# The dense feed-forward of layer 0 as Strassen's seven half-size products, with the weight sums made on VectorE

## The reference, cut to what matters

```python
D_MODEL = 1024
D_FF = 2816

def swiglu(h, wg, wu, wd):
    return (jax.nn.silu(h @ wg) * (h @ wu)) @ wd

    # layer_forward, layer 0: x = x + gt2 * swiglu(h2, w_ff_gate, w_ff_up, w_ff_down)
```

## Time and profile before

| | |
|---|---|
| time, median of 3 runs | 1638.91 us (1638.71 to 1642.12) |
| span of the profiled execution | 1643.6 us |
| TensorE busy in it | 1601.4 us (97%) |
| VectorE, ScalarE, GpSimd busy | 414.5, 150.2, 69.6 us |
| memory traffic | 535 MB, mean 326 GB/s |

### The profile page before, as it was taken

One profiled execution on the slowest core, in us unless ns is written; L12 is line 12 of the kernel. 1 busy time (PEld: TensorE's weight loads), 2 busy tenths in 40 slices (PEclk: granted clock), 3 DMA queues, 4 the chain that ended last, 5 costly groups with the idle time before them and its releaser, 6 DMA issues.

```text
span 1643.6 us, 34513 instructions
## 1 busy us (share of the span) xinstructions
PE 1601.4 (97%) x15756; PEld 1002.9 (61%) x15756; DVE 414.5 (25%) x877; ACT 150.2 (9%) x364; POOL 69.6 (4%) x118
## 2 busy tenths in 40 slices
PE   7999999999999999999999999999999999999997
PEld 3778887888886888863444444444554555555544
DVE  4468353101103794441111001100110011011132
ACT  2102301000002112130000000000000000000000
POOL 1111500000000010001000000000000000000010
PEclk8999999999999999999999999999999999999999
DMA  9998878564348877348999999999999999999995
GB/s 364 365 374 303 284 255 258 163 201 145 123 159 285 272 256 230 128 134 343 404 418 418 404 417 404 418 418 404 418 416 404 412 393 418 418 399 418 411 386 186
DMA packets 188920, 535.14 MB, mean 326 GB/s; under 512 B 13047, under 2 KB 113189, under 8 KB 175970
## 3 DMA queue, kind: packets, MB, share of 16 engines
q1 hardware_dynamic: 173298, 497.20, 79.9%
q0 software_dynamic: 8768, 28.96, 5.0%
q10 hardware_dynamic: 6704, 6.72, 1.3%
HBM read 517.47 MB, written 15.82 MB: 324 GB/s over the span
## 4 chain that ended last, share of the span: by engine, by line
PE 81%; DMA 12%; DVE 4%; SPq 1%; issue 1%; ACT 0%; POOL 0%; DVEq 0%
PE bank L1465 30%; PE bank L1486 14%; PE bank L1109 11%; PE bank L1022 10%; DMA ring<-in_w_exp_up 9%; PE bank L1322 5%; PE bank L1298 3%; PE bank L1286 2%; PE bank L1030 1%; DMA ring<-in_w_ada 1%; DVE inv L1922 1%; DMA w_route<-in_w_router 1%; PE bank L1273 1%; SPq L591 1%; PE bank L1124 1%
## 5 line engine op out<-in xcount | busy, mean ns | idle before, releaser
L1465 PE MATMUL bank<-ring,area 128*32 128x448 f32 x3072 | 302.9, 539 | 3.5 <-DMA ring<-in_w_exp_up 3.2
L1465 PE MATMUL bank<-ring,xT 128*32 128x448 f32 x3072 | 301.7, 539 | 3.6 <-DMA ring<-in_w_exp_up 3.4
L1109 PE MATMUL bank<-hT,ring 128*128 128x264 f32 x1024 | 239.3, 389 | 0.8 <-ACT hT L814 0.8
L1486 PE MATMUL bank<-area 128*32 128x256 f32 x3840 | 227.8, 379 | 1.2 <-issue 1.0
L1109 PEld LDWEIGHTS bank<-hT,ring 128*128 128x128 f32 x1024 | 193.4, 191 | 36.4 <-issue 4.5
L1465 PEld LDWEIGHTS bank<-ring,area 128*32 128x32 f32 x3072 | 109.8, 110 | 165.0 <-issue 157.8
L1465 PEld LDWEIGHTS bank<-ring,xT 128*32 128x32 f32 x3072 | 111.0, 110 | 162.6 <-issue 154.7
L1486 PEld LDWEIGHTS bank<-area 128*32 128x32 f32 x3840 | 139.2, 110 | 100.0 <-issue 44.3
L496 DVE TENSOR_TENSOR area<-bank,area 128x448 f32<-128x448 f32 x48 | 45.9, 956 | 577.5 <-ACT area L981 577.5
L1022 PE MATMUL bank<-hT,ring 128*128 128x264 f32 x704 | 157.4, 386 | 0.0
L1022 PEld LDWEIGHTS bank<-hT,ring 128*128 128x128 f32 x704 | 133.7, 190 | 23.2 <-issue 0.4
(11 more groups left out here) (314 smaller groups left out, 882.1 us busy)
## 6 DMA issues: line engine op xcount, KB each, us to landing
ring<-in_w_exp_gate SPq DMA_DIRECT2D x128, 896.0 KB, 18.2
ring<-in_w_exp_up SPq DMA_DIRECT2D x128, 896.0 KB, 20.0
area<-in_w_exp_down SPq DMA_DIRECT2D x64, 1024.0 KB, 18.3
ring<-in_w_ada SPq DMA_DIRECT2D x96, 512.0 KB, 10.4
ring<-in_w_in SPq DMA_DIRECT2D x32, 1024.0 KB, 12.5
ring<-in_w_exp_down SPq DMA_DIRECT2D x32, 1024.0 KB
area<-in_w_exp_down SPq DMA_DIRECT2D x32, 512.0 KB
ring<-in_w_ff_gate SPq DMA_DIRECT2D x22, 512.0 KB, 7.3
```

The costliest lines, as they stand in the source:

```text
L1109: mm = pe.matmul(bank[b][:, 0:T], w[:, c, :], hT[:, c, :], start=(c == 0), stop=(c == DC - 1))
L1465: mm = pe.matmul(bank[t + 3 * half][32 * g:32 * g + 32, 0:SLICE], tokens[:, t, 32 * r:32 * r + 32], w[half][:, SLICE * g:SLICE * (g + 1)], ...
L1486: mm = pe.matmul(bank[6 + t // 2][32 * q:32 * q + 32, (t % 2) * S:(t % 2 + 1) * S], FFN["actT"][:, m % 2, t, 32 * i:32 * i + 32], wide(at) ...
```

## The change: what it does

The two matrices of each product are cut in halves both ways: 256 hidden channels (two chunks) by 1024 input channels, and the tokens into 2 x 132. Four quarter products of each quarter of the result need 8 half-size products; the seven of Strassen's scheme (in Winograd's form) do with sums of quarters as operands. A half-size product has 128 x 128 weights over 132 tokens. Output columns come in `units` of two chunks: unit 2i is gate chunks 2i and 2i+1, unit 2i+1 the same of up (22 units of 7 products of 4 matmuls), and 4 units of the down product (7 products of 11 matmuls), which contracts all 22 hidden chunks at once, so that the groups and `fT` are gone. Before it was 16 matmuls over 264 tokens for each gate or up unit and 44 for each down unit.

Products of a unit are numbered 1, 2, 5, 6, 3, 7 and the fourth; `left(u)` and `right(u)` are the two banks of unit u, 132 columns each, one of three pairs. 1, 6, 7 and the fourth accumulate in `left`, 2 alone and then 5 and 3 in `right`; VectorE and ScalarE take partial sums out in between. VectorE makes three sums of weight quarters into `w_sum` and a fourth over its place in the page (`sum_pair` for a pair of units, `sum_down` for a down unit), one pair ahead, and once the four sums of `hT` quarters (`h_sum`, in `sq`) and three or four of the activations (`act_sum`). Gate, up and down pages come two at a time. The read of `mod` for layer 1 moves a little. Layer 1's first modulation waits for 14 of the 16 `x_new`, its sums of squares use bank 2 instead of 1, and ScalarE no longer waits for all of `x_new` before it starts the norm of layer 1. Some semaphores are shared now; one of these adds a wait: VectorE's bias rows at the start also wait for the constants' transfer.

```diff
-FF_GROUPS = (6, 6, 5, 5)
+HALF = T // 2
+DOWN_UNITS = 4
...
+                for j in range(0, FF_CHUNKS, 2):
+                    for kind, w in (("gate", A["w_ff_gate"][0]), ("up", A["w_ff_up"][0])):
+                        yield (kind, l, j), cols(w, j, 2)
+                        yield (kind, l, j + 1), None
+                for j in range(DOWN_UNITS):
+                    for q in range(3):
+                        rows = slice(q * DC * P, min((q + 1) * DC, FF_CHUNKS) * P)
+                        yield ("down", l, 6 * j + 2 * q), cols(A["w_ff_down"][0][rows, :], 2 * j, 2)
+                        yield ("down", l, 6 * j + 2 * q + 1), None
...
# TensorE
+            def product(out, w, x, first, last=True):
+                n = len(w)
+                for c in range(n):
+                    mm = pe.matmul(out, w[c], x[c], start=(first and c == 0), stop=(last and c == n - 1), skip_group_check=True)
+                return mm
...
+                def five_six(u):
+                    w5, w6 = summed(u // 2, 0), summed(u // 2, 1)
+                    pe.wait_ge(s.w_summed, 4 * (u // 2) + 1)
+                    pe.wait_ge(s.c11_read, u + 1)
+                    if u == 0:
+                        pe.wait_ge(s.h_summed, 1)
+                    product(right(u), [w5[:, u % 2, c, :] for c in range(4)], with_sums(0), True).then_inc(s.product_mm, 1)
...
+                    pe.wait_ge(s.w_summed, 4 * (u // 2) + 2)
+                    pe.wait_ge(s.one_kept, u + 1)
...
+                def fourth(u):
+                    pe.wait_ge(s.c22_read, u + 1)
...
+                first_two(0)
+                first_two(1)
+                five_six(0)
+                three_seven(0)
+                five_six(1)
+                fourth(0)
+                for u in range(1, FF_UNITS - 1):
+                    first_two(u + 1)
+                    three_seven(u)
+                    five_six(u + 1)
+                    fourth(u)
...
+                for u in range(a, a + DOWN_UNITS):
+                    down_middle(u)
+                    if u + 2 < a + DOWN_UNITS:
+                        down_pages(u + 2)
+                        down_one(u + 2, every)
+                    down_fourth(u)
+                    if u + 2 < a + DOWN_UNITS:
+                        down_two(u + 2, every)
...
# VectorE
+                        a11, a12, a21, a22 = v[:, 0:4, 0:P], v[:, 4:8, 0:P], v[:, 0:4, P:2 * P], v[:, 4:8, P:2 * P]
+                        if k == 0:
+                            r = dve.tensor_tensor(out, a21, a22, ALU.add)
+                        elif k == 1:
+                            r = dve.tensor_tensor(out, s1, a11, ALU.subtract)
+                        elif k == 2:
+                            r = dve.tensor_tensor(out, a12, s2, ALU.subtract)
+                        else:
+                            r = dve.tensor_tensor(a21, a11, a21, ALU.subtract)
...
+                for k in range(4):
+                    sum_pair(0, k)
+                b11, b12, b21, b22 = hs[:, 0:4, 0:HALF], hs[:, 0:4, HALF:T], hs[:, 4:8, 0:HALF], hs[:, 4:8, HALF:T]
+                dve.wait_ge(s.h_ready, 2 * DC)
+                for k, x, y in ((0, b12, b11), (1, b22, h_sum[:, 0, :, :]), (2, b22, b12), (3, b21, h_sum[:, 1, :, :])):
+                    if k in (1, 3):
+                        dve.wait_ge(s.h_summed, 1 + k // 2)
+                    dve.tensor_tensor(h_sum[:, k, :, :], x, y, ALU.subtract).then_inc(s.h_summed, 1)
+                read11(0, FF0["got_c"][:, 0, 0, 0:HALF])
+                for i in range(FF_PAIRS):
+                    u, g = 2 * i, FF0["got_c"][:, i % 2, :, :]
...
+                    read11(u + 1, even[:, 0:HALF])
+                    if i:
+                        more(0)
+                    read12(u, g[:, 0, HALF:T])
+                    read22(u, g[:, 1, HALF:T])
+                    if i == 0:
+                        more(0)
+                    more(1)
+                    if i < FF_PAIRS - 1:
+                        read11(u + 2, FF0["got_c"][:, (i + 1) % 2, 0, 0:HALF])
+                    more(2)
+                    read12(u + 1, even[:, HALF:T])
+                    read22(u + 1, odd[:, HALF:T])
...
+                    step(dve.tensor_tensor(even, even, g[:, 0, :], ALU.mult))
...
+                    step(dve.tensor_tensor(odd[:, HALF:T], odd[:, HALF:T], g[:, 1, HALF:T], ALU.mult))
+                    step(dve.tensor_tensor(act_sum[:, i, 0, :], even[:, HALF:T], even[:, 0:HALF], ALU.subtract))
+                    step(dve.tensor_tensor(act_sum[:, i, 2, :], odd[:, HALF:T], even[:, HALF:T], ALU.subtract))
+                    step(dve.tensor_tensor(act_sum[:, i, 1, :], odd[:, HALF:T], act_sum[:, i, 0, :], ALU.subtract))
+                    more(3)
+                    last_quarter(i)
...
# layer 1
                 if l:
+                    pe.wait_ge(s.x_new, DC + DC - 2)
                     for n in range(16, 24):
                         modulation(1, n, 0)
```

More of the change, by code:

```diff
@@ L302, in build @@
         DOWN_ROWS = ((0, 1), (2, 3), (4, 5), (6,), (7, 8), (9, 10), (11,), (12, 13))
-        PAIRED = ("z", "branch", "out")
-        SUM_BANK = (1, 3, 1, 7)
+        PAIRED = ("z", "branch", "out", "gate", "up", "down")
+        SUM_BANK = (1, 3, 2, 7)
         BIAS_BANK = (6, 7, 1, 5)
@@ L379, in used_up, with pages_at, summed, down_summed @@
             return number[(kind, l, i)] + 1
+        def pages_at(kind, i):
+            at, count = arrives[number[(kind, 0, i)]]
+            return pair_cols(at), page_in[at], count
+        def summed(i, k):
+            at = 4224 * (i % 2) + 1024 * k
+            return w_sum[:, at:at + 1024].rearrange("p (u c n) -> p u c n", u=2, c=4)
+        def down_summed(j, k):
+            at = 4224 * (1 - j % 2) + FF_PAIRS * P * k
+            return w_sum[:, at:at + FF_PAIRS * P].rearrange("p (c n) -> p c n", c=FF_PAIRS)
+        def product_order():
+            yield from ((1, 0), (2, 0), (1, 1), (2, 1), (5, 0), (6, 0), (3, 0), (7, 0), (5, 1), (6, 1))
+            for u in range(1, FF_UNITS - 1):
+                yield from ((1, u + 1), (2, u + 1), (3, u), (7, u), (5, u + 1), (6, u + 1))
+            first = FF_UNITS
+            yield from ((3, first - 1), (7, first - 1), (1, first), (2, first), (1, first + 1), (2, first + 1))
+            for u in range(first, first + DOWN_UNITS):
+                yield from ((5, u), (6, u), (3, u), (7, u))
+                if u + 2 < first + DOWN_UNITS:
+                    yield from ((1, u + 2), (2, u + 2))
+        finished = {product: n + 1 for n, product in enumerate(product_order())}
+        def left(u):
+            return bank[u % 3][:, 0:HALF]
+        def right(u):
+            return bank[3 + u % 3][:, 0:HALF]
         def experts(dve, step, f, act_t, silu, add_f, read_mod):
@@ L916, in _, with keep_five @@
                     touch(ACT.Silu)
[L917 to L924 removed]
+                    def keep_five(u):
+                        act.wait_ge(s.product_mm, finished[5, u])
+                        if u >= 2:
+                            act.wait_ge(s.c22_read, u - 1)
+                        act.copy(kept5[u % 2], right(u)).then_inc(s.five_kept, 1)
@@ new lines, in keep_two, with keep_one, silu_last @@
+                    def keep_two(u):
+                        act.wait_ge(s.product_mm, finished[6, u])
+                        if u >= 2:
+                            act.wait_ge(s.c12_read, u - 1)
+                        act.copy(kept2[u % 2], left(u)).then_inc(s.two_kept, 1)
+                    def keep_one(u, out):
+                        act.wait_ge(s.product_mm, finished[1, u])
+                        act.copy(out, left(u)).then_inc(s.one_kept, 1)
+                    def silu_last(i):
+                        act.wait_ge(s.pages_used, used_up("gate", 0, 2 * i + 1))
+                        act.activation(FF0["got_c"][:, i % 2, 1, 0:HALF], left(2 * i), ACT.Silu).then_inc(s.silu_out, 1)
@@ L1015, in page, with page_pair @@
                 return slot(n % RING)
[L1017 to L1021, removed]
-                    mm = pe.matmul(out, w[:, c, :], x[:, c, :], start=(c == 0), stop=(c == DC - 1))
-                mm.then_inc(s.pages_used, 1)
+            def page_pair(kind, i):
+                n = used[0]
+                assert stream[n][0] == (kind, 0, i)
+                at, count = arrives[n]
+                pe.wait_ge(page_in[at], count)
+                used[0] += 2
+                return pair_cols(at)
@@ L1962, in _ @@
                 if l == 0:
[L1963 to L1983 removed]
+                    feed_forward()
                 else:
```

439 lines of the change are left out of this document (323 added, 116 removed).

## The result

The changed kernel takes 1621.3 us (median of 4 runs, 1619.38 to 1627.39) against 1638.81 us: a ratio of 0.9897, 95% interval 0.9872 to 0.9922. Forecast were 1617.1, range 1612 to 1627. In a second measurement of both it is 0.9896 (0.9879 to 0.9914). The profiled execution has a span of 1625.7 us, 17.9 less than before's.

What follows compares the result with a forecast made beforehand. TensorE's stream of matmul records bounds the feed-forward: 209.4 + 4.5 + 0.5 + 0.2 = 214.6 against 235.15 us, -20.5, with -1.3 at the end -21.8, so 1638.9 becomes 1617.1 us; range 1612 to 1627.

Steps and rivals of the forecast that it cites:

- The pace: Feed-forward matmuls on TensorE: 1848 records of 132 columns at 0.1133 us each, 209.4 us, read from four records.
- The rival of the load as the pace: Feed-forward: weight loads set the record spacing; slower above 0.125 us each, 1759 us at 0.190; chance 0.11.
- The rule of the Trainium skill: Feed-forward matmuls: load and matmul together set the spacing, giving 0.164 us a record and a stage of 303 us.
- VectorE: Gate and up pairs: 10.4 us of VectorE work hides under TensorE's 12.7; as bound, with late pages, chance 0.09.
- The start: Feed-forward start: TensorE waits 4.5 us before product 5 of unit 0 for VectorE's sums and `read11`.
- The clock: After the feed-forward's starting stall: ten microseconds at half clock lose 5.1 us, time 1622.2; chance 0.30.
- the case without: The forecast itself, no clock fall after the feed-forward's starting stall: 1617.1 us; chance 0.46.
- the wait of 2.2 us at 58 us: Near the kernel's start: a single TensorE wait of 2.2 us that did not take the clock to half.
- Small stalls: Feed-forward: 0.5 us for some 180 hand-overs between TensorE and VectorE, from nothing to above 3 us.
- The end: Feed-forward's end to `z`: -1.3 us from the squares' wait; nothing counted for `z` pages, late by up to 1 us otherwise.
- The squares' wait: Layer 1's modulation: TensorE's 1.29 us wait for ScalarE's squares goes, -1.3 us.
- Given back later: Expert stage: its transfers, at 0.99, set the end and the gain is lost, 1637 to 1639 us; chance 0.04.

Runs made afterwards that it cites:

- The doubled sums: Changed kernel with VectorE making one, or two, weight sums twice per pair of units after the first; 1626.03 and 1636.06 us, one run each.
- the stream of 96 columns: Changed kernel with gate and up products streaming 96 of their 132 columns, part of the result not computed; 1630.5 us in one run.

## Why the prediction was right

**The pace.** Right, and to the point on which all hung: 0.1125 measured against 0.1133, 1848 x 0.1125 = 207.9 against 209.4 us. Four records were, here, enough to read it from. The rival of the load as the pace falls, with a margin that I did not see: at 0.1117 the load is the next bound. The rule of the Trainium skill ("TensorE: Matmul & The Clock Gate", "Back-to-back issue gap"), from which 0.164 came as an estimate, does not hold for these 32-bit passes: the trace has 0.1125.

**VectorE.** Right: no wait in the pairs. Its work is smaller than I said, 134 us in the stretch and not 150. The doubled sums show some 1.8 us in hand in a pair where my sum had 2.3 (12.7 less 10.4): with less work than I said VectorE is nearer to being the bound, so waiting in its order counts too, not its work alone.

**The start.** The wait was 3.8 instead of 4.5 us, and its cause as told.

**The clock.** This is the rival that came true, in smaller size: after the wait the clock fell, but for 3.4 us and not for 10, which costs 1.7 and not 5.1. With the same wait it fell in six of seven profiled executions (for 3.4 or 6.8 us), and in one it did not; I gave 0.30 beside 0.46 for the case without. One argument of mine was chance: that the wait of 2.2 us at 58 us "did not do it". Near there seven of the twelve profiled executions wait for 1.7 to 2.2 us, and in two of them, after waits of 1.82 and 1.94 us, the clock falls. After the change:

```profile
57.90 0.63 PE L1464 MATMUL bank<-cst,area 120*128 120x120 f32 x4 [1.82 <-DMA w_route<-in_w_router]
```
```profile
59.00:62.30 3.30, 3.30 (x30) 1.53 (x23) 0.52 (x3) 0.00 (x0) 0.00 (x0) 0.50 1.07 384
```

**Small stalls.** 0.5 us was said; the last two down units each wait 0.55 us (0.39 of it idle) for `read22`, since no product stands between their seventh and fourth. In the walk through VectorE's order I had looked at pairs and at the length of a down unit, not at this hand-over.

**The end.** Here a step failed, as I put it: "3 MB in the 12 us before `z` starts ... I count nothing; late by up to 1 us otherwise." The squares' wait went as predicted (-1.3), and with GpSimd's loads away the way is 11.8 us. But I did not count GpSimd's loads (1.3 MB), whose release, the last `x_new`, now comes right after the last record instead of after `add_f`. The pages ahead of `z` I counted rightly for the kernel after, four, but misread for the one before: its three were issued before the last record. That alone did not matter: with GpSimd's loads away the four are still issued after the end and `z` waits for `hT` again, and with the slots given back earlier, but the loads where they were, the wait stays. The wait is 4.5 us, and the clock falls after it once more, 1.7 us. In the prediction's own terms the end is +2.4 + 1.7 instead of -1.3, 5.4 us off. The other terms together are 0.5 us off (215.1 against 214.6 for the stretch), and that is luck in part: the shorter pace (1.5) and wait (0.7) stand against the clock (1.7) and the two hand-overs (1.1 where I had 0.5).

So the stages that the change touches give -16.0 us in the profile and not -21.8. The medians differ by 17.5, the spans by 17.9, since the first and the last row of the table add -1.9, which I had no term for and which no run puts down to the change. That the forecast is only 4.2 us off and not nearly 6 is luck as well.

**Given back later.** No: from the fourth `z` column to the experts' part it takes the same to 0.1 us, and the experts' part is not longer.

Open: why the clock stays in one execution out of seven after an equal wait and falls in two of seven after a shorter one; and how much of 3.1 us in the experts' part is more than chance.

## What to carry to other kernels

Halving the columns of a matmul pays only while its stream is longer than the load of its weights: here 132 columns are about the last that do, so seven products of half size win. The same scheme once more inside would not, by an estimate: it needs 1848 x 7/4 = 3234 records of 66 columns, and at 0.1117 us each, the pace of the loads, these take 361 us. When a stage ends earlier for one engine, list every queue that its last semaphore releases, GpSimd's too, and ask what they send at the moment the next stage's pages are due. Where an engine must prepare operands before a stage, let it make them in the order in which they are used.

## What the runs showed of the hardware

A load of 128 x 128 32-bit weights, shown with 190 ns, repeats every 0.1117 us in the stream of 96 columns, under matmuls on the same rows. After waits of 3.8 us with full work on both sides TensorE's granted clock went to its lower level, 1.2 GHz, for 3.4 or 6.8 us in six of seven executions, and at the waits of 4.5 to 5.1 us before `z` in all seven. It fell after shorter waits too, for 3.4 us: once after 2.7 us, and in two of seven executions after 1.7 to 2.2 us. At the kernel's start it was 10.2 us, in other executions of the same work 6.8 or 3.4.
